# Dense computation of the top 2048 rows of both expert tables beside the row gathers

## The reference

```python
s1 = jnp.einsum('thd,hnd->thn', q[:, :, 0], k1)      # 128 first keys
s2 = jnp.einsum('thd,hnd->thn', q[:, :, 1], k2)      # 128 second keys
v1, i1 = lax.top_k(s1, 16);  v2, i2 = lax.top_k(s2, 16)
...
cand_idx = i1[..., :, None] * 128 + i2[..., None, :]
sc, pos = lax.top_k(cand, 16);  idx = take_along_axis(cand_idx, pos)
g = softmax(sc)
act = gelu(jnp.einsum('thkd,td->thk', u[idx], t))    # u: 16384 x 2048, f32
out = jnp.einsum('thk,thkd->td', g * act, v[idx])    # v: 16384 x 2048, f32
```

## Time and profile before

| what | value |
|---|---|
| median of 3 runs | 2830.72 us |
| the profiled execution's own time | 2830.14 us |
| its span, first to last instruction | 2828.4 us |
| TensorE, VectorE, ScalarE, GpSimd busy | 86%, 58%, 34%, 32% of the span |
| DMA, mean over the span | 276 GB/s, 779.47 MB |
| the same in the expert stage | about 421 GB/s |

### The profile page before, as it was taken

The page is one execution under the profiler, slowest core; times in us unless marked ns, Lnnn a source line. Parts: engine busy times, 40 slices in busy tenths (PEclk is TensorE's granted clock), DMA queues, the critical chain, the costliest instruction groups (busy, mean ns, idle before and its releaser), DMA issues.

```text
span 2828.4 us, 28105 instructions
## 1 busy us (share of the span) xinstructions
PE 2446.5 (86%) x10791; PEld 1668.7 (59%) x10791; DVE 1644.0 (58%) x2300; ACT 973.4 (34%) x1595; POOL 894.9 (32%) x731
## 2 busy tenths in 40 slices
PE   8999999999999999999998777777777777777777
PEld 7877898888888888778888322222222322222222
DVE  4767564555456555567556896666644444444444
ACT  5567565544777444455553111000010001000001
POOL 6013150000000000431003665555455544454552
PEclk9999999999999999999999899999999899999999
DMA  7544404555445546334456999999999999999998
GB/s 238 182 149 146 138 16 144 163 199 194 149 134 180 180 128 223 129 119 151 157 170 245 422 421 421 421 422 421 421 422 421 411 421 422 422 421 422 421 421 333
DMA packets 200404, 779.47 MB, mean 276 GB/s; under 512 B 16564, under 2 KB 20880, under 8 KB 134096
## 3 DMA queue, kind: packets, MB, share of 16 engines
q0 software_dynamic: 74400, 537.15, 45.9%
q1 hardware_dynamic: 125872, 240.53, 25.4%
HBM read 775.54 MB, written 2.10 MB: 275 GB/s over the span
## 4 chain that ended last, share of the span: by engine, by line
DMA 36%; PE 25%; DVE 3%; issue 1%; POOL 1%; ACT 1%; DVEq 0%; ACTq 0%
DMA VROW<-in_peer_v_dram,WORK 34%; PE bank L2038 24%; DMA UROW<-in_peer_u_dram,WORK 2%; POOL UROW L592 1%; DVE UROW L1982 1%; POOL VROW L599 1%; DVE BIG L1602 0%; DVE WL L1302 0%; PE bank L2174 0%; ACT WH L718 0%; DVE WL L1308 0%; PE bank L2216 0%; DVE BIG L1600 0%; DVE WORK L1625 0%; DVE BIG L1626 0%
## 5 line engine op out<-in xcount | busy, mean ns | idle before, releaser
L2038 PE MATMUL bank<-VROW,WORK 128*128 128x512 f32 x2028 | 937.9, 608 | 335.1 <-DMA VROW<-in_peer_v_dram,WORK 296.5
L2038 PEld LDWEIGHTS bank<-VROW,WORK 128*128 128x128 f32 x2028 | 370.9, 192 | 901.5 <-issue 747.8
L1982 DVE CUSTOM_DVE_ANT_0 UROW<-UROW,BIG 128x2048 f32<-128x2048 f32 x256 | 586.7, 2293 | 521.3 <-DMA UROW<-in_peer_u_dram,WORK 508.5
L2038 PE MATMUL bank<-HX,WH 128*128 128x512 f32 (+1 forms) x2784 | 759.8, 345 | 12.0 <-issue 4.8
L2038 PE MATMUL bank<-HX,WL 128*128 128x256 f32 x2128 | 595.6, 280 | 0.0
L599 POOL DMA_INDIRECT VROW<-in_peer_v_dram,WORK x256 | 404.1, 1578 | 518.0 <-PE bank L2038 495.8
L2038 PEld LDWEIGHTS bank<-HX,WH 128*128 128x128 f32 x2784 | 479.9, 189 | 84.3 <-issue 16.9
L1308 DVE TENSOR_TENSOR WL<-RAW,WH 128x1024 fp32r<-128x1024 f32 (+2 forms) x261 | 305.2, 1180 | 297.0 <-ACT WH L718 296.1
L2038 PE MATMUL bank<-WH,HX 128*128 128x512 f32 (+1 forms) x1472 | 451.8, 389 | 3.4 <-ACT BIG L661 2.5
L2038 PEld LDWEIGHTS bank<-HX,WL 128*128 128x128 f32 x2128 | 402.4, 189 | 0.1
L592 POOL DMA_INDIRECT UROW<-in_peer_u_dram,WORK x256 | 268.9, 1050 | 242.7 <-DVE WORK L1671 144.6
(11 more groups left out here) (350 smaller groups left out, 1689.9 us busy)
## 6 DMA issues: line engine op xcount, KB each, us to landing
RAW<-in_w_in_odd_dram SPq DMA_DIRECT2D x64, 1024.0 KB, 5.4
RAW<-in_w_in_even_dram SPq DMA_DIRECT2D x48, 1024.0 KB, 5.2
RAW<-in_w_in_dram SPq DMA_DIRECT2D x44, 1024.0 KB, 5.1
RAW<-in_w_out_even_dram SPq DMA_DIRECT2D x16, 1024.0 KB, 5.1
RAW<-in_w_out_odd_dram SPq DMA_DIRECT2D x16, 1024.0 KB, 5.2
RAW<-in_w_out_dram SPq DMA_DIRECT2D x16, 1024.0 KB, 5.0
RAW<-in_peer_wq_dram SPq DMA_DIRECT2D x16, 1024.0 KB, 5.0
UROW<-in_peer_u_dram,WORK POOLq DMA_INDIRECT x256, 26.4
```

What stands on the lines that cost most here:

```text
L1982: dve.tensor_tensor_reduce(out=UROW[:, b, :], in0=UROW[:, b, :], in1=TT, op0=ALU.mult, op1=ALU.add, scale=1.0, scalar=0.0, accum_out=DOT[: ...
L2038: return pe.matmul(dst, lhsT, rhs, start=start, stop=stop, skip_group_check=True)
```

## The change

The 16 first keys 112 to 127 own the rows 14,336 to 16,383 of both tables, 2048 rows of each. These are now loaded whole, in order, and computed for all 256 tokens.

- Gathers: a pick whose index is above 14,335 is out of bounds of the gather (`bounds_check`, no error), which skips it. Its coefficient in the gathered sum is zero (`KEPT_GATE`).
- SyncE loads 16 tiles of 128 rows (1 MB) of the first table and 16 of the second into two buffers `DROW`.
- First table: TensorE transposes a tile in 4 steps of 4 (`dense_turn`), ScalarE copies it to SBUF (`dense_turned`), and TensorE multiplies it with the transposed tokens `HT` (`dense_dots`, 4 products of 256 columns a step). 64 steps, beside rows 2 to 109 of the second table's order. ScalarE's GELU of the 128 x 256 result goes to `ACTED`.
- Gates: for each of 16 groups of 16 tokens VectorE writes 0/1 matrices of both keys in bfloat16 (`one_hots`), TensorE multiplies them in 48 products of 16 columns (`dense_gates`; the gate stands in three bfloat16 parts), and VectorE multiplies `ACTED` with the result (`mix`). These stand beside rows 112 to 158.
- Second table: TensorE multiplies `ACTED` with `DROW`, 64 steps of 2 products of 512 columns (`dense_values`), beside rows 161 to 226. Group 0's sum goes to banks of its own and is added by `add_dense`, group 1's joins the gathered rows' banks.
- The gathers have 4 buffers a table instead of 6.
- VectorE adds 50 whole second-table rows instead of 2: every fourth of rows 7 to 107 (26) and 163 to 247 (22), each 9 picks later in its own order, and the old two.
- Both groups' token rows `TT` are made at the start (before, the second at pick 128), and a dot product waits for the end of the one before.

```diff
-ROWS_EACH = 6
+ROWS_EACH = 4
+DENSE = 16
+KEPT = PE_KEYS - DENSE
-ON_DVE = (N_PICKS - 5, N_PICKS - 3)
+ON_DVE = tuple(v for v in range(4, 108) if v % 4 == 3) + tuple(v for v in range(160, N_PICKS - 8) if v % 4 == 3)\
+    + (N_PICKS - 5, N_PICKS - 3)
+U_AT = spread(U_STEPS + 1, 2, 109)
+G_AT = spread(GROUPS, 112, 158)
+V_AT = spread(V_STEPS, 161, 226)
...
+            for j in range(DENSE):
+                if j >= 2:
+                    sp.wait_ge(s["d_t"], HT_STEPS + 4 * (j - 1))
+                dense_rows("peer_u_2", j, j % 2)
...
                 pool.indirect_dma_start(
                     UROW[:, n % ROWS_EACH, :], None, a["peer_u_2"],
-                    bass.IndirectOffsetOnAxis(ap=PICK[:, n // PICKS, n % PICKS:n % PICKS + 1], axis=0))\
+                    bass.IndirectOffsetOnAxis(ap=PICK[:, n // PICKS, n % PICKS:n % PICKS + 1], axis=0),
+                    bounds_check=KEPT * PE_KEYS - 1, oob_is_err=False)\
...
-                    pool.wait_ge(s["v_used"], v - ROWS_EACH + 1)
+                    before = v - ROWS_EACH
+                    if before in ON_DVE:
+                        pool.wait_ge(s["v_on"], rows_before(ON_DVE, before) + 1)
+                    else:
+                        pool.wait_ge(s["v_used"], rows_before(ON_PE, before) + 1)
                     second_row(v)
...
+            def dense_turn(i):
+                j, g = i // 4, i % 4
+                if g == 0:
+                    pe.wait_ge(s[f"d_row{j % 2}"], 16 * (j // 2 + 1))
+                pe.wait_ge(s["d_tc"], HT_STEPS + max(i - 1, 0))
+                for q in range(4):
+                    c0 = (4 * g + q) * P
+                    ins = pe.transpose(bank[4 + i % 2][:, q * P:(q + 1) * P], DROW[:, j % 2, c0:c0 + P], ID[:, :])
+                ins.then_inc(s["d_t"], 1)
...
+            def dense_gates(g):
+                pe.wait_ge(s["g_in"], g + 2)
+                if g >= 2:
+                    pe.wait_ge(s["g_mix"], g - 1)
+                for t in range(IN_GROUP):
+                    dst = bank[6 + g % 2][:, t * DENSE:(t + 1) * DENSE]
+                    for k in range(3):
+                        ins = mm(dst, OH2[:, g % 2, t, :], OH1[:, g % 2, k, t, :], k == 0, k == 2)
+                ins.then_inc(s["g_g"], 1)
...
+                if n - V_LAG - 1 in ON_DVE:
+                    row_on(n - V_LAG - 1, 0)
```

More of the change, by code:

```diff
@@ L44 @@
 PICKS = PE_HEADS * PE_TOP
-ROWS_EACH = 6
+ROWS_EACH = 4
 V_LAG = 8
+DENSE = 16
+KEPT = PE_KEYS - DENSE
+U_STEPS, V_STEPS = 4 * DENSE, 4 * DENSE
+GROUPS, IN_GROUP = 16, 16
+HT_STEPS = 8
 BATCH = 4
@@ L60, with spread, steps_at, rows_before @@
 GATES_AT = 116
+def spread(steps, first, last):
+    return {i: first + i * (last - first) // steps for i in range(steps)}
+U_AT = spread(U_STEPS + 1, 2, 109)
+G_TURN_AT = 110
+G_AT = spread(GROUPS, 112, 158)
+V_AT = spread(V_STEPS, 161, 226)
+G_PARTS_AT = G_TURN_AT + V_LAG + 1
+OH_AT = {g: v + V_LAG - 1 for g, v in G_AT.items()}
+MIX_AT = {g: v + V_LAG + 2 for g, v in G_AT.items()}
+def steps_at(places, at):
+    return [i for i, p in places.items() if p == at]
+def rows_before(rows, v):
+    return sum(r < v for r in rows)
 V_LN = 0
@@ L614, in _ @@
             second_row(2)
-            pool.wait_ge(s["ws_used"], done + 6)
-            first_row(4)
-            second_row(4)
             pool.wait_ge(s["ws_used"], done + 8)
[L619 to L625, removed]
+            second_row(1)
+            second_row(3)
+            for n in range(ROWS_EACH, N_PICKS + V_LAG):
                 if n < N_PICKS:
@@ L1957, in root, with mix @@
+            def mix(g):
+                dve.wait_ge(s["g_g"], g + 2)
+                dve.wait_ge(s["d_act"], DENSE)
+                gates_of = bank[6 + g % 2][:, 0:IN_GROUP * DENSE].rearrange("p (t a) -> p a t", a=DENSE)
+                for half in range(2):
+                    x = ACTED[half][:, :, IN_GROUP * g:IN_GROUP * (g + 1)]
+                    ins = dve.tensor_tensor(x, x, gates_of[:, 8 * half:8 * half + 8, :], ALU.mult)
+                ins.then_inc(s["g_mix"], 1)
             def root(m):
@@ L2004, in _ @@
                 if n == SCALE_AT:
[L2005 removed]
+                    dve.wait_ge(s["ln_in"], 32)
                     scale(0, 0, D // 2)
@@ new lines, in dense_turn, with dense_dots @@
+            def dense_turn(i):
[6 more added lines that the diff above has]
+                    ins = pe.transpose(bank[4 + i % 2][:, q * P:(q + 1) * P], DROW[:, j % 2, c0:c0 + P], ID[:, :])
+                ins.then_inc(s["d_t"], 1)
+            def dense_dots(i):
+                j, g = i // 4, i % 4
+                pe.wait_ge(s["d_tc"], HT_STEPS + i + 1)
+                if g == 0 and j >= 2:
+                    pe.wait_ge(s["d_act"], j - 1)
+                dst = bank[6 + j % 2][:, 0:T]
+                for q in range(4):
+                    k = 4 * g + q
+                    ins = mm(dst, UT[:, i % 2, q * P:(q + 1) * P], HT[:, k, :], k == 0, k == KT - 1)
+                ins.then_inc(s["d_m"], 1)
@@ new lines, in beside_row @@
+            def beside_row(v):
+                for i in steps_at(U_AT, v):
+                    if i < U_STEPS:
+                        dense_turn(i)
+                    if i >= 1:
+                        dense_dots(i - 1)
+                if v == G_TURN_AT:
+                    gates_turn()
+                for g in steps_at(G_AT, v):
+                    dense_gates(g)
+                for i in steps_at(V_AT, v):
+                    dense_values(i)
+            tokens_turned()
+            for n in range(N_PICKS):
+                if n in ON_DVE:
+                    beside_row(n)
+                    continue
+                k = rows_before(ON_PE, n)
```

235 lines of the change are left out of this document (183 added, 52 removed).

## The result

| | before | after |
|---|---|---|
| median of 5 runs each, us | 2830.9 (2830.5 to 2832.1) | 2846.6 (2842.2 to 2850.5) |
| ratio, 95% interval | | 1.0053 [1.0041, 1.0064] |
| span of the profiled execution, us | 2828.4 | 2844.7 |
| mean granted clock of TensorE | 0.987 | 0.968 |

The change makes the kernel 15.7 us slower. The forecast was 2851 us, so its sign and size came out; the way there did not come out in every term.

A forecast was written before the change was run, and what follows sets the result against it. It took each DMA engine's own speed during the gathers as the bound. 2830.1 - 67 (skipped rows) + 80 (dense tiles) + 9 (VectorE) = 2852, forecast as 2851 us; 8-in-10 range 2778 to 2888.

The forecast's parts named there:

- What bounds the kernel: Gather stage: each DMA engine's own limit, 26.3 GB/s, sets the pace; the engine with the fewest skipped rows finishes last.
- Rival A: Every gather: remaining rows spread evenly over the engines, so bytes decide; 2772 us, or 2792 with lost slack; chance 0.30.
- rival C: Gathers: a skipped row is replaced by a transfer of the same length, so skipping saves nothing; 2920 to 2925 us; chance 0.04.
- Part 1: Gathers' skipped rows: the busiest engine has 7.58 of 8 rows over 32 picks, saving 67 us; bounds 34 and 102.
- Part 2: Dense tiles: 32 loads of 1 MB on the same busy DMA engines cost 80 us; bounds 0 to 80.
- Part 3: TensorE's dense work stays below the gathers' pace, just hidden in the gate part: 0 us.
- Rival B: TensorE's gate part: 768 narrow products at 0.12 us or more, plus handovers, add 19 to 40 us; chance 0.12.
- Part 4: VectorE's added rows and mixing are hidden except in the early stretch, 1586 to 1700 us: +9 us, bounds 0 to 18.
- mark of VectorE over 97% busy: Sign for the early-stretch cost: picks 10 to 36 take 9 us longer, with VectorE over 97% busy.
- Part 5: Gather ring with four buffers: engines don't run dry in a steady stretch, 0 us; bounds 0 to 15.
- Rival D: The ring runs dry: late issues and four buffers cost 15 to 30 us more all over, 2866 to 2881; chance 0.07.
- The signs: Picks 40 to 110: pitch stays near 5 us, DMA share below 1, GB/s below 421; the page's bytes 751 MB.

The follow-up runs named there:

- rows_off_vector: The changed kernel with only the two old second-table rows on VectorE, TensorE taking the other 48: 2833.2 us, ratio 1.0009.
- skip_fourths: The changed kernel skipping, in every gather, partitions p mod 4 = 3 within 0 to 31 and 64 to 95, whatever their pick: 2795.1 us.
- skip_eighths: The changed kernel skipping, in every gather, the 16 partitions with p mod 8 = 3, whatever their pick: 2926.8 us, ratio 1.0336.
- full_rows: The changed kernel with its gathers unbounded, so every row is fetched, skipped picks' rows too: 2926.5 us, ratio 1.0338.
- before_four: The kernel before with four buffers a table instead of six, the changed kernel's gather start, one whole row on VectorE: 2845.2 us, ratio 1.0051.
- thin_tiles: The changed kernel with 30 of the 32 dense tiles loaded with 16 columns only, same products and waits: 2779.3 us, ratio 0.9824.
- freed_earlier: The changed kernel with each row addition of VectorE one pick earlier (8 picks behind instead of 9): 2837.3 us, ratio 1.0022.
- skip_six: The kernel before with only the gathers' bound added, six buffers, no dense part: 2717.5 us, ratio 0.9602.

## Why the prediction was near, and where its terms were off

The experiments let the change be put together in four steps, each the difference of two measured kernels: four buffers +14.4 (2830.7 to 2845.2), skipping -93.6 (to 2751.6), the dense part +81.6 (to rows_off_vector, 2833.2), 48 rows on VectorE +13.4 (to 2846.6). The sum is 15.8, as it must be, since the steps lead from one kernel to the other; in another order single steps could come out otherwise.

- **What bounds the kernel.** Right, and decisive: the single DMA engine's speed, not the chip's. Rival A, even shares, is out: skip_fourths and skip_eighths would have been equal. So is rival C: skipping saves 80 us.
- **Part 1, -67.** The ends of 34 and 102 held, the value was too small: 80.0 measured inside the changed kernel, 93.6 where the dense part isn't there. The step that failed is the assignment of eight neighbouring partitions to an engine (refuted by skip_eighths, 2926.8 us where it gave 2787); by the other assignment the same window of 32 picks gives 75. The window was the other weak part. Windows of the ring's own 8 gathers (4 picks) would give only 38 us by this assignment, and 80 to 94 were measured with four buffers, 113.3 with six (2830.7 to 2717.5), next to the 115 of the whole stage. So the engines even out over far more gathers than the ring holds, and no run says over how many. That it is 93.6 there and 80.0 in the changed kernel has its other side in full_rows, which is only 81.3 above before_four, about the tiles' 33.6 MB at 421.5 GB/s (80). By these differences the rows on VectorE cost next to nothing as long as all rows are fetched, and their 13.4 us appear with the skipping; that was not run by itself.
- **Part 2, +80.** 81.6 for the whole dense part, TensorE's and VectorE's shares of it included; the transfers alone at least 67.2 (thin_tiles, which still loads two tiles and narrow strips). It was right that the tiles get little from the gaps.
- **Part 3, 0.** Right, with more room than I gave it. I took the 16-column product at a pitch of 0.08 us, between 0 and 0.12. The timeline of TensorE in the gate part shows 48 of them in 1.35 us, 0.028 each:

```profile
2146.24 1.35 PE L2209 MATMUL bank<-BIG 128*128 128x16 bf16 x48
```

  768 of these are 22 us, not 61. Picks 110 to 160 need 251.2 us where they needed 250.6. Rival B is out. That TensorE was not at its limit is also the reason why the rows on VectorE had nothing to give.
- **Part 4, +9.** 13.4 measured, inside its bounds of 0 to 18. I had put it into the stretch of picks 10 to 36, where VectorE has too little idle time. By start of the dot products 4.6 us of the 13.4 arise by pick 36, 8.7 by pick 60, and the difference then stays between 7 and 12 (the two profiled executions are 11.3 apart). So about a third of it stands where the step said. The larger share is the buffer given back late (freed_earlier, 9.3, and nothing of it by pick 36: 14.0 us behind the kernel before there, after 13.6), which the step on the buffers named ("freed 9 picks later than its own") and dismissed with "still enough". The forecast's mark of VectorE over 97% busy did not come: 80.88 of 87 us are 93%. Picks 10 to 36 took 136 us after 121, 15 longer instead of 9; before_four has 7 of these 15.
- **Part 5, 0.** Wrong, at the upper end of its bounds: 14.4. The steady stretch was judged rightly. The step failed at the stops: I wrote that a stop of over 10 us would drain four buffers and named the one at pick 128 (13 us), then priced it at nothing. In before_four it takes 6 us, the start 5, the tail 4. The landings were to be 15 to 17 us: 16.5 in before_four and 16.4 in full_rows, as said, and 13.2 in the changed kernel, where rows are skipped and buffers come back late. Rival D has the right mechanism, just below the lower end of its 15 to 30 us, though at the stops, not all over.
- **The signs.** The pitch from pick 40 to 110 stayed at 5.0 and the GB/s fell below 421, both as said; the DMA share fell less than expected in the long stretch (1.00 with 406 GB/s), which a reader should note. The share is the time of the packets' records, and some of these are drawn out: 355 of the gathers' 16,740 packets of 8 KB in that stretch have over 330 ns, up to 2.3 us (before 11 of 18,912, none over 1), 138 us more than at 310 ns each, of 16 x 368 us. The short packets make only 42 us. GB/s is the better sign. The bytes are 751.49 MB, as said.

So the sum came near partly by luck. In the four steps above part 1 was 27 us too small a saving, and parts 2, 4 and 5 together 20 us too small a cost (1.6, 4.4 and 14.4); 6 are left of it, forecast +22 against +15.8.

The last piece is the tail, from the last dot product to the end: 38.9 us against 33.7. The chain in order of time there, with the last gather on it:

```profile
2810.89 10.55 PE bank L2209 x24
...
2822.23 6.51 DMA VROW<-in_peer_v_dram,WORK
...
2828.87 7.10 PE bank L2209 x12
```

24 records in 10.55 us are 0.44 each, at the pitch of the earlier trace rows; the last 12 take 0.59, partly at the lower clock. before_four has 4 of these 5 us in its tail too, at a mean clock of 0.988, so four buffers are probably the main cause.

## What to carry to other kernels

Where a gather's rows are skipped or uneven, count the rows of each DMA engine, not the bytes: the fullest engine is the pace. Its rows over the whole stage bound the gain (115 us here, where the bytes say 147), and a shuffled order (9 to 12 us) or a deeper ring (20 us) brings in part of what is missing from it. Price fewer buffers at the stops (start, change of phase, tail), not in the steady stretch, and price rows moved to another engine by when their buffer comes free. Before work is moved off an engine, look whether that engine was waiting: here TensorE could be 94% busy at no loss.

## What the runs showed of the hardware

- A row beyond an indirect gather's bound leaves a packet of 4 bytes and 9 ns (a row of 8 KB: 309 ns, medians): 7,544 more of these for 7,544 skipped rows (24620 packets under 512 B against 17076 in full_rows).
- The bounds check itself makes an issue on GpSimd 56 ns longer: 937 ns median without it in full_rows, 993 in the changed kernel (first table; 937 before, 990 in skip_six). For 512 issues that is 29 us of GpSimd's time; what it costs the kernel was not run by itself.
- Two kernels with the same 470.07 MB of gathers lie 131.8 us apart, by the partitions alone.
- A product of 16 columns in bfloat16 with its own weights takes 0.028 us in a row of 48 (1.35 us).
